# Hybrid encoder step on one core: another hand-written order for the attention units' scores, scalings, turnings and value products

## What is computed

```python
h = rmsnorm(x, g_norm1)
z = h @ w_in                       # q, k, v of three branches, forget logits, three gates
# retention (4 heads), forgetting attention (8 heads x 64), memory attention (4 heads x 128)
s = einsum('bqhd,bkhd->bhqk', q, k) * scale + decay_bias      # bias only in the forgetting branch
o = einsum('bhqk,bkhd->bqhd', softmax(s), v)
merged = g0 * (o_ret @ w_br_ret) + g1 * (o_fox @ w_br_fox) + g2 * (o_mem @ w_br_mem)
x = x + merged @ w_out
x = x + moe(rmsnorm(x, g_norm2))   # top-1 of 4 groups, top-2 of 8 SwiGLU experts
```

## Time and profile before

| | |
|---|---|
| median of 3 runs | 714.48 us (710.5 to 715.51) |
| profiled execution: its own time | 714.14 us |
| its span, first to last instruction | 712.4 us |
| mean granted TensorE clock | 0.98 |
| PE busy | 674.1 us, 95% of the span |
| DVE, ACT, POOL busy | 361.3, 264.2, 115.2 us |

### The profile page before, as it was taken

How to read it: one execution, slowest core, us unless ns; L and a number is a source line. 1 busy time by engine, 2 the same in 40 slices (tenths; PEclk the granted TensorE clock), 3 DMA queues, 4 the chain that set the end, 5 groups by cost and what they waited for, 6 DMA issues and landing times.

```text
span 712.4 us, 9678 instructions
## 1 busy us (share of the span) xinstructions
PE 674.1 (95%) x3599; PEld 449.4 (63%) x3599; DVE 361.3 (51%) x742; ACT 264.2 (37%) x510; POOL 115.2 (16%) x125
## 2 busy tenths in 40 slices
PE   5999999989999899989899999889999999999995
PEld 4878888778887576767777878544444444543333
DVE  4757449963555454544346751763224443444244
ACT  5573433262443444455934332641212112212101
POOL 0019326660002010000000100020111010112000
PEclk9999999999999899999999999899999999999997
DMA  8957333452126333203857389129999999999952
GB/s 319 387 218 236 119 118 119 132 222 89 60 90 235 111 108 113 66 29 119 315 197 286 125 301 422 72 110 411 405 420 421 421 420 421 420 419 421 421 245 91
DMA packets 32528, 171.95 MB, mean 241 GB/s; under 512 B 4016, under 2 KB 4160, under 8 KB 19296
## 3 DMA queue, kind: packets, MB, share of 16 engines
q1 hardware_dynamic: 30528, 163.29, 59.0%
q0 software_dynamic: 1952, 8.01, 3.3%
HBM read 165.90 MB, written 5.39 MB: 240 GB/s over the span
## 4 chain that ended last, share of the span: by engine, by line
PE 83%; issue 8%; DVE 4%; ACT 4%; POOL 0%; ACTq 0%; DVEq 0%; POOLq 0%
PE banks L1835 15%; PE banks L1493 13%; PE banks L1495 13%; PE banks L1494 13%; PE banks L1859 8%; PE banks L1823 3%; PE banks L1877 2%; PE banks L1870 1%; PE banks L1681 1%; PE banks L1797 1%; PE banks L1766 1%; PE banks L1654 1%; ACT z L907 1%; PE banks L1695 1%; PE banks L1567 1%
## 5 line engine op out<-in xcount | busy, mean ns | idle before, releaser
L1117 DVE TENSOR_TENSOR w_lo<-raw,w_hi 128x1024 fp32r<-128x1024 f32 (+1 forms) x81 | 128.2, 1594 | 85.5 <-ACT w_hi L880 85.3
L1493 PE MATMUL banks<-w_hi,hT_hi 128*128 128x512 f32 x312 | 125.5, 402 | 0.7 <-DVE w_lo L1117 0.6
L1495 PE MATMUL banks<-w_hi,hT_lo 128*128 128x512 f32 x312 | 122.8, 394 | 0.0
L1494 PE MATMUL banks<-w_lo,hT_hi 128*128 128x512 f32 x312 | 122.8, 393 | 0.0
L880 ACT ACTIVATE w_hi<-raw 128x1024 fp32r<-128x1024 f32 x79 | 83.4, 1056 | 88.7 <-PE banks L1495 84.5
L1835 PE MATMUL banks<-wgu,xs 128*64 128x512 f32 x512 | 112.6, 592 | 0.0
L1835 PEld LDWEIGHTS banks<-wgu,xs 128*64 128x64 f32 x512 | 36.7, 137 | 72.7 <-issue 72.7
L1493 PEld LDWEIGHTS banks<-w_hi,hT_hi 128*128 128x128 f32 x312 | 59.6, 191 | 14.5 <-DVE w_lo L1117 1.5
L1495 PEld LDWEIGHTS banks<-w_hi,hT_lo 128*128 128x128 f32 x312 | 59.3, 190 | 12.8
L1494 PEld LDWEIGHTS banks<-w_lo,hT_hi 128*128 128x128 f32 x312 | 59.6, 191 | 11.7
L1859 PE MATMUL banks<-wdn,act_T 128*64 128x512 f32 x256 | 58.5, 598 | 1.6 <-DVE act_T L1314 0.9
(11 more groups left out here) (336 smaller groups left out, 1056.4 us busy)
## 6 DMA issues: line engine op xcount, KB each, us to landing
wgu<-in_wexp SPq DMA_DIRECT2D x64, 1024.0 KB, 14.9
raw<-in_wstream SPq DMA_DIRECT2D x79, 512.0 KB, 3.8
wdn<-in_wexp SPq DMA_DIRECT2D x32, 1024.0 KB, 13.6
foxc<-in_foxc POOLq DMA_DIRECT2D x8, 512.0 KB, 4.0
memv<-in_memc SPq DMA_DIRECT2D x8, 512.0 KB, 4.9
memk<-in_memc SPq DMA_DIRECT2D x8, 512.0 KB, 5.0
xT<-in_xT SPq DMA_DIRECT2D x1, 1536.0 KB, 11.2
xtok<-in_xtok SPq DMA_DIRECT2D x1, 1536.0 KB, 7.8
```

Source lines behind the costliest of these rows:

```text
L1117: dve.tensor_tensor(w_lo[:, i % PART_SLOTS, cols], raw[:, i % RAW_SLOTS, cols], w_hi[:, i % PART_SLOTS, cols].bitcast(F32), ALU.subtract). ...
L1493: mm(out, xh, wh, start=start, stop=False, skip_group_check=True)
L1494: mm(out, xh, wl, start=False, stop=False, skip_group_check=True)
L1495: return mm(out, xl, wh, start=False, stop=stop, skip_group_check=True)
```

## The change

Three edits, all in the list of `schedule()`. First, the first two gate granules (36 and 37) come after turnings 4 and 11 in place of 5 and 12. Second, the attention loop's step i reads: turning of unit i-2, scores of i, the granule if there is one, scaling of i-1, turning back of i-4, value product of i-3, parts. Before it read: scaling of i-1, scores of i, the granule, value product or turning back of i-3, value product of i-2 for `foxs`, turning of i-1, parts. Third, behind the loop, the sigmoids of gates 1 to 5 move: gate 1 now follows the value product of unit 30, gates 2 to 5 follow `merge` of the first branch chunk, and the value product of unit 31 comes before the scores of unit 32.

```diff
     for i in range(20):
         s.append(("turn", i))
-        if i in (5, 12, 19):
+        if i in (4, 11, 19):
             gate()
...
-    oT_parts = {3 + j: j for j in range(4)} | {last_fox + 3 + j: 4 + j for j in range(4)}
+    oT_parts = {3 + j: [j] for j in range(4)} | {last_fox + 4: [4], last_fox + 5: [5], last_fox + 6: [6, 7]}
+    assert last_fox + 6 < early
     for i in range(early):
+        if i >= 2:
+            pieces.append(("unit_p", i - 2))
+        pieces.append(("unit_s", i))
         if i >= 1:
             pieces.append(("unit_w", i - 1))
-        pieces.append(("unit_s", i))
-        for j in (i - 3,):
-            if 0 <= j:
-                pieces.append(("unit_v" if units[j][0] in ("foxp", "memp") else "unit_o", j))
-        for j in (i - 2,):
-            if 0 <= j and units[j][0] in ("foxs", "mems"):
-                pieces.append(("unit_v", j))
-        if i >= 1:
-            pieces.append(("unit_p", i - 1))
-        if i in oT_parts:
-            pieces.append(("parts", oT_parts[i]))
+        if i >= 4 and units[i - 4][0] in ("foxs", "mems"):
+            pieces.append(("unit_o", i - 4))
+        if i >= 3:
+            pieces.append(("unit_v", i - 3))
+        pieces += [("parts", j) for j in oT_parts.get(i, [])]
...
     n, r = early, FIRST[C_BR]
-    s += [("mem_caches",), ("unit_w", n - 1), ("unit_v", n - 3), ("gates", 0), ("gates", 1)]
+    s += [("mem_caches",), ("unit_p", n - 2), ("unit_w", n - 1), ("unit_v", n - 3), ("gates", 0)]
     granule(r)
-    s += [("gates", 2), ("unit_p", n - 1), ("unit_v", n - 2)]
+    s += [("unit_p", n - 1), ("unit_v", n - 2), ("gates", 1)]
     granule(r + 1)
-    s += [("gates", 3), ("gates", 4), ("gates", 5)]
     merge(r + 1)
-    s += [("unit_s", n)]
+    s += [("gates", 2), ("gates", 3), ("gates", 4), ("gates", 5), ("unit_v", n - 1), ("unit_s", n)]
     granule(r + 2)
-    s += [("unit_v", n - 1), ("unit_w", n), ("unit_s", n + 1)]
+    s += [("unit_w", n), ("unit_s", n + 1)]
```

## The result

The changed kernel takes 725.47 us (median of 4 runs, 722.42 to 728.04), the kernel before 714.36 us (4 runs, 710.5 to 715.51). The ratio is 1.0163, with a 95% interval of 1.0132 to 1.0195: slower by 1.6%. The profiled execution took 722.42 us, the fastest of the four, with a span of 720.6 us and a mean granted clock of 0.983; the others had 0.980, 0.980 and 0.976 and spans of 723.7, 723.7 and 726.3 us. So the runs of one kernel differ by their clock, and the trace shows the change with 3 us less than its median. The source is three lines shorter, so line L1681 of before is L1678 here, L1212 is L1209, L1493 is L1490.

A forecast was written before the change was run, and what follows sets the result against it. The prediction took the kernel as a queue of PE work, PE being busy 95% of the span. Its terms summed as 714.14 + 9.5 + 0 - 2.1 - 0.5 + 4 = 725 us, with an 8-in-10 range of 715 to 733.

The forecast's parts named there:

- The extra step that does not exist on PE, and the scaling that moved instead: In the loop, turning keeps its place on PE; scaling on DVE moves behind the maximum of the next scores.
- Ungated positions: 17 loop places without a granule: PE waits for the scaling, 17.6 us where 8.1 stood, +9.5 us.
- The sign that I gave: Turnings waiting for the scaling rise from 4 waits to about 14, some 0.9 us each, 12 to 14 us total.
- Gated positions: 14 loop places with a granule: chain of 4.4 us covered by 4.7 us of PE work, so 0.
- Behind the loop, -2.1: Wait for bank 0 shrinks from 1.85 to about 0.7 us, slow stretch may go, about 1 us given back.
- Turnings, -0.5: Granule 36 starts some 1.7 us sooner, but turning 10 waits for a copy, giving 1.2 back: -0.5 us.
- The clock, +4: In the loop, about four half-clock stretches of 2 us each, 8 us in all: about 4 us more.
- Same work behind the loop, no term: Everything behind 381 us (merging, routing, experts) only shifts by the sum and has the same work: no term.
- The rival "faster": In the loop, DVE freed from waiting for the exponential starts every exponential sooner: 699 us, half of it 706; chance 0.06.
- The rival that the clock stays and the time is 719 us: Loop waits come as worked out, but half clock stays at its two stretches or vanishes: 719 us; chance 0.27.

The follow-up runs named there:

- (1): Changed kernel with the scaling put back in front of the scores: 707.80 us, ratio 0.9908 to the kernel before.
- Variant 8: Changed kernel with the scaling directly behind the maximum, in front of the granule's low part: 723.58 us, ratio 1.0150 to the kernel before.
- (3): Kernel before with only the new order behind the loop, old loop and turnings kept: 712.42 us, ratio 0.9971.
- (4): Kernel before with only the first two granules among the turnings placed one turning sooner: 712.36 us, ratio 0.9961.
- variant 2: Kernel before with only the new loop body, the leftover turning of unit 30 put behind the loop: 732.32 us, ratio 1.0223.

## Why the prediction was right

The forecast was 725 us and the median is 725.47. The mechanism was right, and each step can be held against its own number. That the two agree to half a us is luck in part: single runs lay between 722.42 and 728.04 by their clock, and in the pair of profiled executions the span grew by 8.2 us where the steps add up to 10.9.

- **The extra step that does not exist on PE, and the scaling that moved instead**: right. Moving it back (1) takes away 12.7 of the 16.1 us of waits.
- **Ungated positions, +9.5 us, 17.6 instead of 8.1**: measured 16.1 for the scaling and 0.27 + 0.78 behind the evacuations, 17.15 in all, +9.05. By position: unit 21 0.91 (0.95 forecast), samples' scores mostly 1.2 (1.0), unit 5 2.54 (2.65), unit 30 1.09 (1.1), unit 2 1.16 (1.2), units 26 and 28 0.42 and 0.40 (0.45). The twelve places forecast at 1.0 have 12.4 us together (12.0). At units 14 and 23 I was too high, 1.36 instead of 2.0 together, and it was partly another wait than I had named: the turning back of the sample unit waited there for the rows that ACT copies behind the evacuation. The sign that I gave, about 14 waits and 12 to 14 us, was below my own sum; it is 16 waits and 16.1 us.
- **Gated positions, 0 with 0.3 us to spare**: the chain measured 4.34 us to the scaled row (4.4 with the hand-over), and PE came 0.38 us after it. Variant 8 moved 14 scalings in front of the low part and won nothing that can be told from the noise.
- **Behind the loop, -2.1**: in the trace -2.57 between granules 60 and 79 (12.05 to 9.48). The wait was 0.41 and not 0.7, the half-clock stretch went, and about 0.45 us (9.03 to 9.49) was given back at granule 64, where I had put 1. Alone (3) the whole edit measured 3 us; its trace has 3.0 of its 3.8 us behind the loop, and the table does not split it reliably.
- **Turnings, -0.5**: -0.25 in the trace, with both waits that I had named: 0.82 for bank 0 and 0.88 for the copy of turning 5. Alone (4) it measured -3.0 us, nearly all of it clock; my step had no such term.
- **The clock, +4**: a size that I could not derive, and the step with the least behind it. In the profiled loop the windows lose 8.5 us at half clock against 5.1 before (differences of the clock from 1, times 4 us each), +3.4, and part of that lies inside waits; the loop grew by 12.0 us of which 9.05 are waits, which leaves 3. Over whole runs the table gives +1.7. With only the loop changed it is +9. So +4 lies inside what was seen, but its size was a guess that came out, and it is no property of this change alone. The range rested mostly on it, rightly.
- **Same work behind the loop, no term**: the profiled execution gained 1.3 us there by the clock. That is one part of why the trace shows +8.2 in the span while the medians show +11.1; the other is that the profiled execution is the fastest of the four.

The rival "faster" rested on DVE no longer waiting for the exponential. DVE did stop waiting for it, and that bought nothing. The rival that the clock stays and the time is 719 us was too low for the medians, though the profiled execution at 722.42 came near to it.

The rule of the Trainium skill that I had set against this term (TensorE: Matmul & The Clock Gate, section "HAM oscillation", long gaps only) is not borne out here: half clock came in the changed kernel during or right behind gaps of PE of 0.80, 1.13 and 2.54 us. Its section "A second HAM failure mode: psum-queue depth-cycling", small idles between groups, points the right way: the four versions with 16 short waits lost 13.4 to 21.9 us, the kernel before 10.7 to 12.8. But variant 2 and the changed kernel have the same waits in their loops and lost 21.9 and 14.5, so the section does not give a size.

What stays open: what decides at which of the short waits the clock falls, and with it why 0.3 us won among the turnings takes 3.6 us of clock loss away. The kernel before by itself lost 10.7 to 12.8 us in the three groups.

## What to carry to other kernels

In a hand-written order that all engines share, ask for each moved step which engines have work in it. A step may keep its place on one engine and lose it on another: here the turning did not move on PE, but the scaling that it needs moved behind a maximum that needs PE's newest result, and PE then had to sit out a whole round trip (1.43 us at unit 21), less the little work it had there, at every place without a granule as cover. To find what such a change costs, compute chain less cover place by place; to gain by it, move the consumer by one unit too, or, better here, move what only blocks the queue (the parts: 5.5 us, roughly half of it clock) behind what the bottleneck waits for.

## What the runs showed of the hardware

The clock is a cost of its own kind, and it differs between runs of the same program. The changed kernel's four runs have the same instructions and spans from 720.6 to 726.3 us, and the product of span and clock is within 1 us for all of them (708.3, 709.2, 709.2, 708.9). In other versions that product is less steady, with up to 5 us between runs (variant 3). The median loss differs between versions by up to 17.7 us (21.9 for the loop alone, 4.2 with the turning later), about as much as the rest (693.1 to 709.1). And half clock does not need a long gap: in the kernel before it began 0.9 us behind a wait of 0.96 us (that wait ended at 273.59; second row), while behind the wait of 1.47 us, which ended at 309.45, the clock stayed full (last row).

```profile
273.50:274.50 1.00, 0.91 (x4) 1.00 0.00 0
274.50:277.50 3.00, 3.00 (x9) 0.51 0.00 0
309.45:313.00 3.55, 3.55 (x17) 1.00 0.00 0
```

Nor is it the surroundings of one wait alone: the wait of 1.21 us at the scores of unit 19, the same in two versions, had half clock behind it in variant 2 and full clock in the changed kernel.
